# Expert down products of an MoE layer: weight tiles standing in two 64-column halves, the result transposed back by TensorE

## The chip, the cores and the metric

The kernel runs on one core of one Trainium2 chip. The metric is the device time of one execution in microseconds (us). TensorE is called PE below, its weight loads PEld, VectorE DVE, ScalarE ACT, GpSimd POOL and SyncE SP. "The queue" is the chain of DMA transfers that SP issues.

## The reference

Two layers of a decoder trunk over 256 tokens of width 1024, all in float32. Each layer mixes tokens (a gated DeltaNet half and a stick-breaking attention half, which the change doesn't touch) and then mixes channels: a dense SwiGLU in layer 0, and in layer 1 eight expert SwiGLUs of width 3584, of which each token uses two.

```python
def swiglu(x, w_gate, w_up, w_down):
    return (jax.nn.silu(x @ w_gate) * (x @ w_up)) @ w_down

def moe_swiglu(h, router_w, w_gate, w_up, w_down):
    ...
    logits = (xt @ router_w).astype(jnp.float32)
    top_val, top_idx = lax.top_k(logits, TOP_K)
    gates = jax.nn.softmax(top_val, axis=-1)
    combine = jnp.einsum("nk,nke->ne", gates, jax.nn.one_hot(top_idx, N_EXPERTS, dtype=jnp.float32))
    y = jnp.zeros((B * T, D), dtype=jnp.float32)
    for e in range(N_EXPERTS):
        y = y + combine[:, e:e + 1] * swiglu(xt, w_gate[e], w_up[e], w_down[e]).astype(jnp.float32)
    return y.reshape(B, T, D).astype(h.dtype)
```

The three weight matrices of an expert hold 3 x 1024 x 3584 float32 values, 44 MB; all eight together 352 MB, and every one of them is read.

## The kernel before

The program is written engine by engine, with semaphores between them. Layer 0, the mixer of layer 1 and the router take the first 40% of the time. Then the experts run, in the order of their number. Each expert gets up to 96 tokens (`SLOTS`); if some expert had more, another round over all experts would follow, which happens once here.

**Gather.** `gather` builds the expert's input transposed, `xgT` (eight blocks of 128 features by 96 tokens), as products of three bf16 parts of the activations with one-hot matrices; DVE scales and copies it out of PSUM in `gathered`.

**Chunks.** The expert's width is cut in 14 chunks (`MOE_CH`) of 256 hidden features (`FC`). One chunk's weights are 1 MB each of gate, up and down (`load_ffn`, three transfers). They land in a ring of four slots (`NSLOT`). SP issues the loads of chunk n once the semaphore `ring_used` says that chunk n-4 has been used up, that is, once its down products are done.

**Gate and up, `m_gate_up`.** Weights stand, activations move: a 128 x 64 piece of the weights is the standing operand and the 96 tokens of `xgT` the moving one. The two 64-column halves of a 128-column weight tile go to the two halves of the PE's columns (`for lo in (0, P // 2)`). That makes 64 calls of a chunk. A float32 call is carried out as two MATMUL instructions, each with its LDWEIGHTS, so a chunk has 128 pairs. The result is the hidden layer transposed: features on partitions, 96 tokens along the row.

**Activation.** ACT takes silu of the gate half (L1132), DVE multiplies with the up half (L1505) into `moe_hid`, which is double buffered.

**Down, `m_down`.** Here it is the other way round: the hidden layer (128 features x 96 tokens) stands, and the down weights move, 512 columns at a time:

```python
ins = mm(bank(2 + half)[0:SLOTS, :], moe_hid[c % 2][:, i, :],
         d[:, i, half * 512:(half + 1) * 512], ...)
```

That is four calls, eight MATMULs of 512 columns, in a chunk. The sums of all 14 chunks pile up in PSUM banks 2 and 3, with tokens on 96 partitions and 1024 output features along the row.

**Order on PE.** `expert` runs gate/up of chunk c, then down of chunk c-1, so that ACT and DVE have the time of one down to make the next hidden tile. After gate/up of the last chunk comes the gather of the next expert, then the last down. ACT and DVE then each copy one bank of the result to `y_tok` (`y_copy`, L1125 and L1489), and after gate/up of the next expert's chunk 0, `scatter` spreads the 96 rows back to the 256 token rows by a product with a one-hot matrix (L873, four calls). DVE multiplies with the gate and adds (`accumulate`, L1494).

**Loop.** Expert 0 and expert 7 are written out; between them a loop of three rounds has two experts in its body. The chain of engines at the end of the program is: last `y_copy`, `scatter`, `accumulate`, then norm, residual and the store of the output.

Of the kernel before, what the change touches and what calls it, by code (L numbers as in the profile page):

```python
# [30 lines left out]
P = 128  # L31
D = 1024
# [84 lines left out]
def build(nc, x_in, consts, norm_mix_pre, norm_mix_post, norm_ffn_pre, norm_ffn_post, w_in, conv_w,  # L117
          dn_a_log, dn_dt_bias, dn_norm_w, sb_norm_w, w_out, ffn_gate, ffn_up, ffn_down, router_w,
          moe_gate, moe_up, moe_down, out):
    with ExitStack() as ctx:  # L120
# [90 lines left out]
        def cols(n):  # L211
# [37 lines left out]
        y_tok = BM[0:SLOTS, D:2 * D]  # L249

# [46 lines left out]
            sem(n) for n in ("mgu_ps", "msg_ready", "mhid_ready", "y_act", "y_dve", "scatter_ps"))  # L297
        moe_acc = [sem(f"moe_acc{t}") for t in range(TT)]
# [139 lines left out]
        def _(pe):  # L438
# [413 lines left out]
            def m_down(it, j, c, tail=False):  # L852

                d = gate_up_down(FIRST_MOE + j * MOE_CH + c)[2]
                pe.wait_ge(mhid_ready, it * (2 * MOE_CH) + (j * MOE_CH + c + 1))
                if tail and c == 0:
                    pe.wait_ge(y_act, it * 2 + j)
                    pe.wait_ge(y_dve, it * 2 + j)
                for i in range(FC // P):
                    for half in range(2):  # L860
                        ins = mm(bank(2 + half)[0:SLOTS, :], moe_hid[c % 2][:, i, :],  # L861
                                 d[:, i, half * 512:(half + 1) * 512],
                                 start=(c == 0 and i == 0), stop=(c == MOE_CH - 1 and i == 1))
                ins.then_inc(ring_used, 1)

# [11 lines left out]
            def expert(it, j, tail, nxt):  # L877

                for c in range(MOE_CH):
                    m_gate_up(it, j, c)  # L880
                    if c:
                        m_down(it, j, c - 1, tail)
                    if tail and c == 0:
                        scatter(*tail)
                if nxt:
                    if tail:
                        for t in range(TT):
                            pe.wait_ge(moe_acc[t], it * 2 + j)
                    gather(*nxt)
                m_down(it, j, MOE_CH - 1)  # L890
# [3 lines left out]
            with pe.Fori(0, rounds) as r:  # L894
# [9 lines left out]
                for t in range(TT):  # L904
                    pe.wait_ge(moe_acc[t], last * 2 + 1)
                scatter(last, 1)
# [5 lines left out]
        def _(act):  # L912
# [208 lines left out]

            def y_copy(it, j):

                act.wait_ge(ring_used, it * (2 * MOE_CH) + (FIRST_MOE + (j + 1) * MOE_CH))
                A(y_tok[:, 0:512], bank(2)[0:SLOTS, :], ACT.Copy).then_inc(y_act, 1)  # L1125

            def expert(it, j, tail, nxt):
                for c in range(MOE_CH):
                    act.wait_ge(mgu_ps, it * (2 * MOE_CH) + (j * MOE_CH + c + 1))
                    if c >= 2:  # L1130
                        act.wait_ge(mhid_ready, it * (2 * MOE_CH) + (j * MOE_CH + c - 1))
                    A(moe_sg[c % 2], bank(c % 2)[:, 0:2 * SLOTS].rearrange("p (a b) -> p a b", a=2),  # L1132
                      ACT.Silu).then_inc(msg_ready, 1)
                if nxt:
                    onehotT_copy(*nxt)
                y_copy(it, j)

            with act.Fori(0, rounds) as r:
# [8 lines left out]
                expert(last, 1, (last, 0), None)  # L1147
            for t in range(TT):
# [5 lines left out]
        def _(dve):  # L1154
# [331 lines left out]

            def y_copy(it, j):
                dve.wait_ge(ring_used, it * (2 * MOE_CH) + (FIRST_MOE + (j + 1) * MOE_CH))
                V.tensor_copy(y_tok[:, 512:D], bank(3)[0:SLOTS, :]).then_inc(y_dve, 1)  # L1489
# [10 lines left out]
            def expert(it, j, tail, nxt, nxt_e):  # L1500
                for c in range(MOE_CH):
# [6 lines left out]
                    if tail and c == 0:  # L1508
                        accumulate(*tail)
# [4 lines left out]
                y_copy(it, j)  # L1514

            with dve.Fori(0, rounds) as r:
# [9 lines left out]
                expert(last, 1, (last, 0), None, None)  # L1526
                accumulate(last, 1)
# [180 lines left out]
```

## Time and profile before

| | us |
|---|---|
| three runs: median (lowest to highest) | 1779.08 (1778.29 to 1780.57) |
| the profiled execution, its own time | 1775.79 |
| its span, first to last instruction | 1773.9 |
| PE busy | 1720.2 (97% of the span) |
| PE weight loads busy | 1268.8 (72%) |
| DVE, ACT, POOL busy | 283.3, 197.6, 143.5 |

The time of the profiled execution is 1.9 us more than its span, and 3.3 us less than the median of the three runs. The mean granted clock of TensorE is 0.982 of full speed. A busy PE is no proof of a PE at its peak: the instructions overlap, and what matters is the distance from one start to the next. The DMA share is the mean busy share of the core's 16 DMA engines as the profile counts their packets; it can read slightly over 1 when packets overlap.

### The profile page before, as it was taken

The numbers are of one execution on the slowest core, as the hardware profiler recorded it, in microseconds if no ns is written. First come the engines' busy times: TensorE is split into PE (matmuls) and PEld (weight loads), VectorE is DVE, ScalarE is ACT, GpSimd is POOL, SyncE is SP. The second block draws the span as 40 slices with busy tenths as digits, with TensorE's granted clock in tenths as the row PEclk, the third lists the DMA queues.
The fourth block names the chain that finished last, engine by engine and source line by source line (L and its number), as shares of the span: only waits on it lengthen the run. The fifth ranks groups of instructions, "written<-read, shape, count | busy, mean of one in ns | idle before, by whom it ended". The sixth has DMA issues, their size and how long they took to land.

```text
span 1773.9 us, 41158 instructions
## 1 busy us (share of the span) xinstructions
PE 1720.2 (97%) x18812; PEld 1268.8 (72%) x18812; DVE 283.3 (16%) x553; ACT 197.6 (11%) x462; POOL 143.5 (8%) x164
## 2 busy tenths in 40 slices
PE   7999999999999995999999999999999999999997
PEld 6788577777778755777777776777776777777774
DVE  2333310000434334001001001001001001001002
ACT  3123220000322323000000000000000000000000
POOL 2233200000123322000000000000000000000000
PEclk9999999999999996999999999999999999999999
DMA  8213244443320324999999999899899899899892
GB/s 308 73 46 120 95 152 168 168 153 132 122 102 27 119 95 143 308 350 341 315 350 333 322 351 326 296 349 353 304 350 346 278 348 352 303 352 354 298 353 97
DMA packets 311445, 432.58 MB, mean 244 GB/s; under 512 B 9051, under 2 KB 263261, under 8 KB 311277
## 3 DMA queue, kind: packets, MB, share of 16 engines
q1 hardware_dynamic: 310396, 427.75, 69.9%
q8 instruction: 150, 2.46, 0.6%
q0 software_dynamic: 672, 2.14, 0.4%
q10 hardware_dynamic: 208, 0.08, 0.0%
q14 instruction: 19, 0.15, 0.0%
HBM read 428.90 MB, written 1.05 MB: 242 GB/s over the span
## 4 chain that ended last, share of the span: by engine, by line
PE 94%; DVE 2%; ACT 1%; issue 1%; POOL 1%; SPq 0%; DMA 0%; DVEq 0%
PE ps L848 34%; PE ps L861 23%; PE ps L751 8%; PE ps L488 7%; PE ps L762 3%; PE ps L629 3%; PE ps L497 3%; PE ps L873 2%; PE ps L600 1%; PE ps L615 1%; PE ps L826 1%; PE ps L611 1%; PE ps L621 1%; PE ps L512 1%; PE ps L519 1%
## 5 line engine op out<-in xcount | busy, mean ns | idle before, releaser
L848 PEld LDWEIGHTS ps<-bv_sb,ring 128*64 128x64 f32 x14336 | 598.1, 137 | 92.6 <-issue 92.6
L848 PE MATMUL ps<-bv_sb,ring 128*64 128x96 f32 x14336 | 619.0, 247 | 6.2 <-issue 5.6
L861 PE MATMUL ps<-ring,LT_sb 128*96 128x512 f32 x896 | 410.9, 601 | 0.0
L861 PEld LDWEIGHTS ps<-ring,LT_sb 128*96 128x96 f32 x896 | 137.0, 163 | 191.6 <-issue 179.3
L1505 DVE TENSOR_TENSOR LT_sb<-LT_sb,ps 128x192 f32<-128x192 f32 x112 | 39.7, 354 | 916.8 <-ACT LT_sb L1132 916.8
L751 PE MATMUL ps<-hT_sb,ring 128*128 128x256 f32 (+1 forms) x768 | 155.7, 362 | 0.0
L751 PEld LDWEIGHTS ps<-hT_sb,ring 128*128 128x128 f32 x768 | 136.0, 190 | 24.6 <-issue 9.1
L1132 ACT ACTIVATE LT_sb<-ps 128x192 f32<-128x192 f32 x112 | 37.0, 330 | 948.9 <-PE ps L848 948.9
L488 PE MATMUL ps<-hT_sb,ring 128*128 128x256 f32 x608 | 139.4, 388 | 0.0
L488 PEld LDWEIGHTS ps<-hT_sb,ring 128*128 128x128 f32 x608 | 117.6, 196 | 17.0 <-DVE qk_sb L1220 0.5
L1556 POOL TENSOR_SCALAR small<-small 128x1 f32<-128x1 f32 x16 | 4.1, 254 | 1346.3 <-ACT XT_sb L951 1320.5
L762 PE MATMUL ps<-ring,LT_sb 128*128 128x512 f32 x144 | 64.7, 592 | 0.0
L629 PE MATMUL ps<-ring,hT_sb 128*128 128x512 f32 x128 | 56.7, 593 | 1.7 <-ACT hT_sb L1080 1.7
L497 PE MATMUL ps<-ring,hT_sb 128*128 128x512 f32 x128 | 56.9, 592 | 0.0
L762 PEld LDWEIGHTS ps<-ring,LT_sb 128*128 128x128 f32 x144 | 27.4, 190 | 26.8 <-issue 25.8
L1610 POOL TENSOR_TENSOR BM<-LT_sb,cst 128x512 f32<-128x512 f32 x28 | 37.9, 1365 | 73.5 <-DVE LT_sb L1310 40.5
L629 PEld LDWEIGHTS ps<-ring,hT_sb 128*128 128x128 f32 x128 | 23.5, 190 | 28.0 <-issue 28.0
L497 PEld LDWEIGHTS ps<-ring,hT_sb 128*128 128x128 f32 x128 | 23.7, 190 | 25.9 <-issue 25.8
L1409 DVE TENSOR_TENSOR LT_sb<-AT_sb,ps 128x256 f32<-128x256 f32 x22 | 9.3, 421 | 200.2 <-ACT AT_sb L1092 200.2
L1092 ACT ACTIVATE AT_sb<-ps 128x256 f32<-128x256 f32 x22 | 8.4, 383 | 198.4 <-PE ps L751 198.4
L873 PE MATMUL ps<-BM,X_sb 96*128 96x512 f32 x64 | 29.6, 605 | 0.9 <-DVE BM L1489 0.9
L1220 DVE SCALAR_TENSOR_TENSOR qk_sb<-ps,prm,qk_sb 128x255 f32<-128x255 f32 (+2 forms) x48 | 23.1, 481 | 31.0 <-ACT qk_sb L991 29.9
(259 smaller groups left out, 1002.9 us busy)
## 6 DMA issues: line engine op xcount, KB each, us to landing
ring<-in_moe_w_gate SPq DMA_DIRECT2D x112, 1024.0 KB, 5.9
ring<-in_moe_w_up SPq DMA_DIRECT2D x112, 1024.0 KB, 8.9
ring<-in_moe_w_down SPq DMA_DIRECT2D x112, 1024.0 KB, 10.8
ring<-in_ffn_w_gate SPq DMA_DIRECT2D x11, 1024.0 KB, 5.3
ring<-in_ffn_w_up SPq DMA_DIRECT2D x11, 1024.0 KB, 7.9
ring<-in_ffn_w_down SPq DMA_DIRECT2D x11, 1024.0 KB, 9.8
ring<-in_w_in SPq DMA_DIRECT2D x14, 768.0 KB, 6.4
ring<-in_w_out SPq DMA_DIRECT2D x8, 768.0 KB, 5.5
```

The source lines that it names most:

```text
L488: ins = mm(o[:, 0:T], w[:, k, col:col + P], hT[:, k, :], start=(k == 0), stop=(k == KD - 1))
L497: ins = mm(o, hT[:, k, i * P:(i + 1) * P], w[:, k, col:col + 512], start=(k == 0), stop=(k == KD - 1))
L629: ins = mm(bank(4 + 2 * t + hf), mixT[:, k, t * P:(t + 1) * P], w[:, k, :], start=(k == 4), stop=(k == 3))
L751: ins = mm(bank(mt % 4)[:, which * T + lo:which * T + hi], w[:, k, i * P:(i + 1) * P], hT[:, k, lo:hi], start=(k == 0), stop=(k == KD - 1))
L762: ins = mm(bank(4 + 2 * t + half), ffn_hid[:, mt % 4, t * P:(t + 1) * P], d[:, i, half * 512:(half + 1) * 512], start=(mt == 0), stop=(mt ...
L848: ins = mm(o[lo:lo + P // 2, :], w[:, k, i * P + lo:i * P + lo + P // 2], xgT[:, k, :], start=(k == 0), stop=(k == KD - 1))
L861: ins = mm(bank(2 + half)[0:SLOTS, :], moe_hid[c % 2][:, i, :], d[:, i, half * 512:(half + 1) * 512], start=(c == 0 and i == 0), stop=(c = ...
L873: ins = mm(bank((6, 4)[t] + half), onehotT[j][:, t * P:(t + 1) * P], y_tok[:, half * 512:(half + 1) * 512], start=True, stop=True)
L1132: A(moe_sg[c % 2], bank(c % 2)[:, 0:2 * SLOTS].rearrange("p (a b) -> p a b", a=2), ACT.Silu).then_inc(msg_ready, 1)
L1220: V.scalar_tensor_tensor(conv_dst(m)[:, s:T], bank(step_bank(m + 1))[:, 0:T - s], prm[:, w:w + 1], conv_dst(m)[:, s:T], ALU.mult, ALU.add)\
L1505: V.tensor_tensor(moe_hid[c % 2], moe_sg[c % 2], bank(c % 2)[:, 2 * SLOTS:4 * SLOTS].rearrange("p (a b) -> p a b", a=2), ALU.mult).then_in ...
L1610: G.tensor_tensor(BT[:, s, :], LT[:, s, :], bcm(cst[:, C_LVL + l * P:C_LVL + (l + 1) * P], 4), ALU.mult).then_inc(BT_ready, 1)
```

## The change

The down products take the form of the gate/up products. Each 128 x 64 piece of the down weights stands, in two 64-column halves, and the 96 tokens of `moe_hid` move. Eight blocks of 128 output features times two halves times two feature tiles make 32 calls, 64 MATMULs of 96 columns, in a chunk, instead of 8 of 512 columns. The sums pile up transposed: banks 2 and 3 hold four blocks each of 128 output features by 96 tokens.

The scatter still wants tokens on partitions. So at an expert's end ACT and DVE copy banks 2 and 3 to a new view `yT` of the tile `hT_sb` (`yT_copy`), PE transposes the eight blocks into banks 4 and 5 (`y_transposes`, after gate/up of chunk 0 of the next expert), and ACT and DVE copy those to `y_tok`. The scatter comes one chunk later than before, behind the down of chunk 0, and DVE's accumulation with it. The last expert does all of it in a row.

```diff
+        yT = v3(hT_sb, KD, 0, KD * SLOTS)
...
                 if tail and c == 0:
-                    pe.wait_ge(y_act, it * 2 + j)
-                    pe.wait_ge(y_dve, it * 2 + j)
+                    pe.wait_ge(yT_act, it * 2 + j)
+                    pe.wait_ge(yT_dve, it * 2 + j)
                 for i in range(FC // P):
-                    for half in range(2):
-                        ins = mm(bank(2 + half)[0:SLOTS, :], moe_hid[c % 2][:, i, :],
-                                 d[:, i, half * 512:(half + 1) * 512],
-                                 start=(c == 0 and i == 0), stop=(c == MOE_CH - 1 and i == 1))
+                    for m in range(KD):
+                        o = bank(2 + m // 4)[:, m % 4 * SLOTS:(m % 4 + 1) * SLOTS]
+                        for lo in (0, P // 2):
+                            ins = mm(o[lo:lo + P // 2, :], d[:, i, m * P + lo:m * P + lo + P // 2], moe_hid[c % 2][:, i, :],
+                                     start=(c == 0 and i == 0 and m % 4 == 0), stop=(c == MOE_CH - 1 and i == 1),
+                                     skip_group_check=True)
                 ins.then_inc(ring_used, 1)
+
+            def y_transposes(it, j):
+
+                pe.wait_ge(yT_act, it * 2 + (j + 1))
+                pe.wait_ge(yT_dve, it * 2 + (j + 1))
+                for m in range(KD):
+                    ins = nc.tensor.transpose(bank(4 + m // 4)[0:SLOTS, m % 4 * P:(m % 4 + 1) * P], yT[:, m, :], ident)
+                ins.then_inc(yT_ps, 1)
...
                     if tail and c == 0:
+                        y_transposes(*tail)
+                    if tail and c == 1:
                         scatter(*tail)
...
+                y_transposes(last, 1)
                 scatter(last, 1)
...
+            def yT_copy(it, j):
+
+                act.wait_ge(ring_used, it * (2 * MOE_CH) + (FIRST_MOE + (j + 1) * MOE_CH))
+                A(yT[:, 0:4, :], bank(2)[:, 0:4 * SLOTS].rearrange("p (a b) -> p a b", a=4), ACT.Copy).then_inc(yT_act, 1)
+
             def y_copy(it, j):
 
-                act.wait_ge(ring_used, it * (2 * MOE_CH) + (FIRST_MOE + (j + 1) * MOE_CH))
-                A(y_tok[:, 0:512], bank(2)[0:SLOTS, :], ACT.Copy).then_inc(y_act, 1)
+                act.wait_ge(yT_ps, it * 2 + (j + 1))
+                A(y_tok[:, 0:512], bank(4)[0:SLOTS, :], ACT.Copy).then_inc(y_act, 1)
...
+            def yT_copy(it, j):
+                dve.wait_ge(ring_used, it * (2 * MOE_CH) + (FIRST_MOE + (j + 1) * MOE_CH))
+                V.tensor_copy(yT[:, 4:8, :], bank(3)[:, 0:4 * SLOTS].rearrange("p (a b) -> p a b", a=4)).then_inc(yT_dve, 1)
...
                     if tail and c == 0:
+                        y_copy(*tail)
+                    if tail and c == 1:
                         accumulate(*tail)
```

PE's own order at the start of an expert, before. L848 is gate/up, L873 the scatter, L861 the down product; counts are calls, each two MATMULs.

```order
L898 UNCONDITIONAL_BRANCH
L898 ISA
L839 ISA
L848 MATMUL ps<-bv_sb,ring 64x96 x64
L868 ISA
L873 MATMUL ps<-BM,X_sb 128x512 x4
L848 MATMUL ps<-bv_sb,ring 64x96 x64
L855 ISA
L861 MATMUL ps<-ring,LT_sb 96x512 x4
L848 MATMUL ps<-bv_sb,ring 64x96 x64
```

The same place on PE after the change. L850 is gate/up, L875 the transposes, L865 the down product, L885 the scatter.

```order
L912 UNCONDITIONAL_BRANCH
L912 ISA
L841 ISA
L850 MATMUL ps<-bv_sb,ring 64x96 x64
L872 ISA
L875 MATMUL ps<-cst,hT_sb 96x128 x8
L850 MATMUL ps<-bv_sb,ring 64x96 x64
L857 ISA
L861 REGISTER_ALU
L865 MATMUL ps<-LT_sb,ring 64x96 x32
L885 MATMUL ps<-BM,X_sb 128x512 x4
L850 MATMUL ps<-bv_sb,ring 64x96 x64
```

The four calls of a down product have become 32, and the scatter has moved from before the gate/up of chunk 1 to behind the down of chunk 0, so the slot of chunk 0 is given back ahead of the scatter.

## Rows read from the trace of the kernel before

**Rows 1.** The page: PE's busy tenths and the DMA share in 40 slices.

```profile
PE   7999999999999995999999999999999999999997
DMA  8213244443320324999999999899899899899892
```

**Rows 2.** The page: the chain that ended last, by line.

```profile
PE ps L848 34%; PE ps L861 23%; PE ps L751 8%; PE ps L488 7%; PE ps L762 3%; PE ps L629 3%; PE ps L497 3%; PE ps L873 2%; PE ps L600 1%; PE ps L615 1%; PE ps L826 1%; PE ps L611 1%; PE ps L621 1%; PE ps L512 1%; PE ps L519 1%
```

**Rows 3.** The page: costliest groups (count, then busy us, mean ns, then idle before).

```profile
L848 PEld LDWEIGHTS ps<-bv_sb,ring 128*64 128x64 f32 x14336 | 598.1, 137 | 92.6 <-issue 92.6
L848 PE MATMUL ps<-bv_sb,ring 128*64 128x96 f32 x14336 | 619.0, 247 | 6.2 <-issue 5.6
L861 PE MATMUL ps<-ring,LT_sb 128*96 128x512 f32 x896 | 410.9, 601 | 0.0
```

**Rows 4.** The waits of SP, the issuer of the loads (total, times, longest).

```profile
SPq L402 <- PE ps L861: 680.8, 108, 34.8
```

**Rows 5.** Timeline of one chunk in mid-expert (start, length, engine, group).

```profile
1004.64 5.50 PE L848 MATMUL ps<-bv_sb,ring 128*64 128x96 f32 x128
...
1004.88 0.37 SPq L402 DMA_DIRECT2D ring<-in_moe_w_gate  x1
...
1010.08 3.67 PE L861 MATMUL ps<-ring,LT_sb 128*96 128x512 f32 x8
...
1010.64 0.35 DVE L1505 TENSOR_TENSOR LT_sb<-LT_sb,ps 128x192 f32<-128x192 f32 x1 [8.68 <-ACT LT_sb L1132]
...
1013.68 5.50 PE L848 MATMUL ps<-bv_sb,ring 128*64 128x96 f32 x128
```

**Rows 6.** Timeline, PE: the first two gate/up blocks of expert 0, back to back.

```profile
698.96 10.78 PE L848 MATMUL ps<-bv_sb,ring 128*64 128x96 f32 x256 [0.63 <-DVE bv_sb L1483]
```

**Rows 7.** Timeline, PE: a change of experts inside the loop body.

```profile
1224.40 3.62 PE L861 MATMUL ps<-ring,LT_sb 128*96 128x512 f32 x8
1227.95 5.50 PE L848 MATMUL ps<-bv_sb,ring 128*64 128x96 f32 x128
1233.38 3.70 PE L873 MATMUL ps<-BM,X_sb 96*128 96x512 f32 x8
1237.02 5.50 PE L848 MATMUL ps<-bv_sb,ring 128*64 128x96 f32 x128
```

**Rows 8.** Timeline, PE: the first gate/up block behind the loop's branch back.

```profile
1094.42 6.90 PE L848 MATMUL ps<-bv_sb,ring 128*64 128x96 f32 x128 [2.77 <-issue]
```

**Rows 9.** Windows (engines' busy us, then PE clock, DMA share, GB/s).

```profile
1088.00:1104.00 16.00, 13.22 (x147) 9.22 (x145) 2.33 (x4) 1.30 (x3) 0.00 (x0) 0.89 1.08 371
1005.00:1077.00 72.00, 72.00 (x1088) 52.00 (x1085) 2.83 (x8) 2.64 (x8) 0.00 (x0) 1.00 1.02 350
```

**Rows 10.** A load onto an idle queue: issue, first data (window), landing of its last part.

```profile
1114.15 0.37 SPq L402 DMA_DIRECT2D ring<-in_moe_w_gate  x1
...
1115.00:1116.00 1.00, 1.00 (x30) 1.00 (x28) 0.00 (x0) 0.00 (x0) 0.00 (x0) 1.00 0.62 143
...
L404 SPq DMA_DIRECT2D ring<-in_moe_w_down x1: 1062/1062/1062, 1115.3 to 1115.3; - x1
...
DMA to landing us min/median/max: 10.6/10.6/10.6
```

**Rows 11.** The third parts of two loads queued one behind the other, with their landing.

```profile
L404 SPq DMA_DIRECT2D ring<-in_moe_w_down x1: 3217/3217/3217, 1492.6 to 1492.6; - x1
...
DMA to landing us min/median/max: 11.7/11.7/11.7
...
L404 SPq DMA_DIRECT2D ring<-in_moe_w_down x1: 3657/3657/3657, 1500.5 to 1500.5; - x1
...
DMA to landing us min/median/max: 13.6/13.6/13.6
```

**Rows 12.** Timeline, PE: four transposes in the mixer.

```profile
641.26 0.60 PE L635 MATMUL ps<-cst,h_sb 128*128 128x128 f32 x4
```

**Rows 13.** Timeline, PE: the last scatter of the program.

```profile
1759.78 3.67 PE L873 MATMUL ps<-BM,X_sb 96*128 96x512 f32 x8 [0.87 <-DVE BM L1489]
```

More of the change, by code:

```diff
@@ L297, in build @@
             sem(n) for n in ("mgu_ps", "msg_ready", "mhid_ready", "y_act", "y_dve", "scatter_ps"))
+        yT_act, yT_dve, yT_ps = (sem(n) for n in ("yT_act", "yT_dve", "yT_ps"))
         moe_acc = [sem(f"moe_acc{t}") for t in range(TT)]
@@ L1133, in expert @@
                       ACT.Silu).then_inc(msg_ready, 1)
+                    if tail and c == 0:
+                        y_copy(*tail)
                 if nxt:
                     onehotT_copy(*nxt)
-                y_copy(it, j)
+                yT_copy(it, j)
             with act.Fori(0, rounds) as r:
@@ L1147, in _ @@
                 expert(last, 1, (last, 0), None)
+                y_copy(last, 1)
             for t in range(TT):
@@ L1485, in gathered @@
                                     bcl(wffn[:, 4 * b:4 * b + 4], SLOTS), ALU.mult).then_inc(xg_ready, 1)
+            def yT_copy(it, j):
+                dve.wait_ge(ring_used, it * (2 * MOE_CH) + (FIRST_MOE + (j + 1) * MOE_CH))
+                V.tensor_copy(yT[:, 4:8, :], bank(3)[:, 0:4 * SLOTS].rearrange("p (a b) -> p a b", a=4)).then_inc(yT_dve, 1)
             def y_copy(it, j):
-                dve.wait_ge(ring_used, it * (2 * MOE_CH) + (FIRST_MOE + (j + 1) * MOE_CH))
-                V.tensor_copy(y_tok[:, 512:D], bank(3)[0:SLOTS, :]).then_inc(y_dve, 1)
+                dve.wait_ge(yT_ps, it * 2 + (j + 1))
+                V.tensor_copy(y_tok[:, 512:D], bank(5)[0:SLOTS, :]).then_inc(y_dve, 1)
             def accumulate(it, j):
@@ L1508, in expert @@
                     if tail and c == 0:
+                        y_copy(*tail)
+                    if tail and c == 1:
                         accumulate(*tail)
@@ L1513, in expert @@
                     gathered(*nxt)
-                y_copy(it, j)
+                yT_copy(it, j)
             with dve.Fori(0, rounds) as r:
@@ L1526, in _ @@
                 expert(last, 1, (last, 0), None, None)
+                y_copy(last, 1)
                 accumulate(last, 1)
```

## The prediction

> **What bounds the kernel now.** I read the slices first: from slice 17 on, the experts' part, PE is at 9 tenths and so is the DMA share [rows 1]. Two resources look full, so the question is which one PE would meet if it got faster. The chain that ended last is PE alone there, 34% gate/up (L848) and 23% down (L861) [rows 2]. PE hardly waits: the 14336 gate/up MATMULs have 6.2 us of idle time before them in all, the down MATMULs 0.0 [rows 3]. SP on the other hand waits 680.8 us, 108 times, for down products to free a slot [rows 4]. So PE bounds this part and the loads follow it.
>
> The timeline gives a chunk's price. Gate/up starts at 1004.64, down at 1010.08, the next gate/up at 1013.68 [rows 5]: 5.44 + 3.60 = 9.04 us. Two gate/up blocks back to back take 10.78 us for 256 MATMULs [rows 6]; less the 0.25 us of a single one that is 10.53 / 255 = 41.3 ns from start to start, 5.28 us for 128. The other 0.16 us of the 5.44 is the turn from 64-column tiles to full width.
>
> The loads: a window with two loads queued moves 371 GB/s at a share of 1.08, the mid-expert window 350 GB/s at 1.02 [rows 9]. A chunk is 3.146 MB. At 371 GB/s it takes 8.48 us, and PE asks for one every 9.04 us. The queue has 6% to spare and no more. That is the number to keep in view.
>
> **The change, part by part.**
>
> *Down products.* 64 MATMULs of 96 columns replace 8 of 512. No row shows this operation, but gate/up has its exact form: 128 x 64 standing, 96 moving, two halves in turn. The near end is 41.3 ns each: 64 x 41.3 ns = 2.64 us in place of 3.60. Both turns of tile width go too. The far end is a pair of halves that don't overlap, 82.5 ns each, 5.28 us. I take 41.3, since only the order of the output regions differs. A chunk then costs PE 192 x 41.3 ns = 7.92 us, 1.12 less. Over 112 chunks that would be 125 us.
>
> The standing operand is where a rule speaks against the change. The row: 14336 weight loads keep PEld busy for 598.1 us [rows 3], 41.7 ns each, no slower than the MATMULs. The Trainium skill (TensorE: Matmul & The Clock Gate, section LDWEIGHTS) puts a weight load at its columns over 1.2 GHz, 53 ns for 64 columns; one after another, 192 of them would make a chunk 10.2 us and the kernel slower than before by some 130 us as an estimate. The trace disagrees for the same form already, so the sum doesn't use it.
>
> *Cover of the hidden tile.* DVE ends at 1010.99, 0.91 us behind the start of down [rows 5]; down still covers this with 2.64 us.
>
> *Change of experts.* Before: an expert inside the loop body lasts 1227.95 - 1094.42 [rows 7, 8] = 133.53 us, 1.47 of which is the first block's slowness behind the branch (6.90 against the usual 5.43). 132.06 less 14 x 9.04 leaves 5.5: the scatter takes 3.64 (1233.38 to 1237.02 [rows 7]) and the gather some 2.0. Added are eight transposes. Four take 0.60 us [rows 12], so 0.11 us each; eight cost 0.9, with their turns of width and latency I take 1.4 (bounds 0.9 and 2.5). The `yT` copies lie beside the 5.28 us of gate/up of chunk 0, the `y_tok` copies beside that of chunk 1; each is one pass of ACT and DVE under 0.7 us, free unless gate/up shrank below that. DVE's accumulation moves behind the down of chunk 0; waiting for it are hid 2 (covered by the next gate/up) and the next gather, ten chunks later. SP has no more to issue than before. PE's work of an expert becomes 14 x 7.92 + 2.0 + 3.6 + 1.4 = 118.0 us, for 132.1.
>
> *Branch back.* The loop goes back twice, with 2.77 us idle and 1.47 us of slow start [rows 8]; the granted clock of that window is 0.89 against 1.00 elsewhere [rows 9], some of it at the lower level, 1.2 GHz, behind the idle time. I keep 4.3 each.
>
> *The loads.* They were hidden; now they aren't. 14 x 8.48 = 118.7 us of queue time for an expert stands against 118.0 of PE, and the two don't fall together: in mid-expert the queue needs 8.5 for each 7.92 of PE, and at a change PE is busy elsewhere while the ring is full. What I need is the queue's pace over a long full stretch, which the trace shows for two loads at most. The low bound is 8.48. Of eight such couples the landings lie 8.4 to 8.7 us apart in six; one of the two others is 1492.6 + 11.7 = 1504.3 and 1500.5 + 13.6 = 1514.1, 9.8 apart [rows 11]. All eight average 8.9. The upper bound is 9.04, the pace it keeps today. I take 8.6, near the six, a little up for stragglers and for the instructions that PE fetches through the same engines, 192 pairs a chunk where there were 136.
>
> *The sum of the expert part.* If the queue never rests: first slot free at 698.96 + 2 x 5.28 + 2.64 = 712.2. From there to first data 1.6 us: 0.24 from the last down to SP's issue [rows 5], and some 1.3 from issue to data (1114.15, data from about 1115.4 [rows 10]). 108 loads x 8.6 = 928.8, to 1642.6. From there to landing 1.9: this load took 1115.3 + 10.6 - 1114.15 = 11.8 us in all [rows 10], less 1.3 and 8.6. Behind the last landing one gate/up and two downs, 10.6. Total 1655.1.
>
> Does the queue rest? Only at a change of experts, where slots come free late. Count from the landing of chunk 13. The next load began 1.9 earlier, and four are on order (slots freed by downs 10 to 13), so the queue is full until 4 x 8.6 - 1.9 = 32.5, and with the one behind them until 41.1. PE does gate/up 13, down 12, gather, down 13 (12.6), then gate/up 0, transposes, gate/up 1, down 0 (14.6, at 27.2: in time), then scatter, gate/up 2, down 1 (11.6, at 38.7), data 1.6 later at 40.3. That is 0.8 to spare, and a branch back of 4.3 us costs 3.5, twice. The last down ends at 1662.1.
>
> The PE-only sum for comparison: 699.0 + 112 x 7.92 + 7 x 7.0 + 8.6 = 1643.7. The queue is later. Within an expert PE runs ahead first: a load onto an idle queue takes 12.1 us of the 15.8 that two chunks of PE give it, and the 3.7, with what the pause at the change adds, are used up at 0.7 us a chunk. Then PE waits.
>
> *The end.* Before, the copies start at 1758.94 (0.84 before the scatter [rows 13]), one us behind the last down, and 15.0 us follow. Now comes one more hop of 0.87, eight transposes of 0.11, and latency: 2.3 us (bounds 1.8 and 4, since PE may have fallen to the lower clock). Span: 1662.1 + 1.0 + 15.0 + 2.3 = 1680.4. With 1.9 us around it the profiled execution would take 1682.3. The median stood 3.3 above the profiled time, so **1685.6 us**, 5.3% less. The 125 us of PE shrink to 93: the queue takes the rest.
>
> **The rivals.**
>
> *A, the queue keeps up.* Its pace is 8.4 or better over a long stretch, PE stays the bound, with the 1643.7 from above: 1643.7 + 18.3 + 5.2 = 1667. For it: 371 GB/s is the mean of a window with dips, and single microseconds read up to 410. Against: a share of 1.08 already. The Trainium skill (HBM Reference, section Specifications) says that a core streaming alone measures about 425 GB/s, 7.4 us a chunk; by that the ring would never run dry and A would be the outcome. Rows 9 show 371 with all engines busy.
>
> *B, the queue is slower than it looks.* At 8.9 us, the mean of the eight couples, 108 x 0.3 = 32 more than the forecast: 1718. At 9.04 it is 108 x 0.44 = 48 more: 1733.
>
> *C, the halves don't overlap, slower than before.* Place: `m_down`, where each half changes its output region at every call, within one PSUM bank, while gate/up stays on a region for eight calls. If that stops the overlap, down costs 5.28 and a chunk 10.56: 112 x 1.52 = 170 more, 7 x 1.4 + 2.3 = 12 more, 1961 us. It turns from gain to loss where the down MATMULs stand more than (9.04 - 0.11 - 5.28) / 64 = 57 ns apart. For it: no row shows alternating regions. Against: the halves alternate in gate/up too and their pace is the streaming time.
>
> *D, no real gain:* that pace at about 57 ns, within 4 us of 1779.
>
> **How the numbers follow.** Forecast 0.57, A 0.17, B 0.19, C 0.05, D 0.02. The likeliest is 1685. The range runs from A with a little off, 1664, to the 8.9 of B, 1720; C, D, the far part of B and a queue with no bound at all stay outside, about 0.15. About 0.2% is what a measurement of this kernel can tell from no change. Faster has 0.94, same 0.01, slower 0.05.
>
> **What would show it.** Right: in mid-expert the issues of L402 stand 8.5 to 8.7 us apart (9.04 before) in the last chunks of an expert and 7.9 in the first ones; PE idles some 0.6 us a chunk before gate/up there, the DMA share has no dips; down MATMULs are 64 in 2.64 us; two stops of 2.8 us at the branch. A would show no idle time before gate/up and dips in GB/s. B shows the idle time in over half of each expert's chunks. C shows down blocks of over 5 us and a DMA share of 0.85. Most in doubt is the queue's pace: 0.1 us there is 10 us of the total.

## The result: 0.35% slower, and the profile after

| | before | after |
|---|---|---|
| median (lowest to highest), us, 5 runs each | 1780.12 (1778.29 to 1780.92) | 1786.53 (1780.79 to 1788.51) |
| profiled execution, its own time; its span | 1775.79; 1773.9 | 1780.79; 1779.0 |
| PE busy, us | 1720.2 | 1637.5 |
| mean granted clock | 0.982 | 0.983 |

The ratio is 1.0035, 95% interval 1.0023 to 1.0046. The forecast was 1685.6 us, with a range of 1664 to 1720. PE has 82.7 us less to do, and the kernel gained nothing. From the page of the changed kernel, the parts that answer to [rows 1], [rows 2] and [rows 3], and the line of the instruction queue (packets, MB, share of the DMA engines):

```profile
PE 1637.5 (92%) x25148; PEld 1441.5 (81%) x25148; DVE 287.7 (16%) x561; ACT 201.5 (11%) x470; POOL 143.4 (8%) x164
...
PE   8999999999999995998998998988998988999996
...
DMA  8213244443320324999999999899899799899893
...
q8 instruction: 201, 3.29, 0.8%
...
PE 90%; issue 6%; DVE 2%; ACT 1%; POOL 1%; DMA 0%; DVEq 0%
...
L850 PE MATMUL ps<-bv_sb,ring 128*64 128x96 f32 x14336 | 634.4, 247 | 38.7 <-issue 37.5
...
L865 PE MATMUL ps<-LT_sb,ring 128*64 128x96 f32 x7168 | 332.7, 247 | 53.0 <-issue 52.9
```

The down MATMULs were 410.9 us with no idle time [rows 3] and are 332.7 us with 53.0. The digits of PE have fallen to 8 in many slices, while DMA has stayed at 9. And the idle time is ended by "issue": PE waited for nothing that the profile shows, no load, no hidden tile, no copy. PE's waits, longest totals first (us in total, times, longest):

```profile
PE ps L865 <- issue: 52.9, 42, 1.9
PE ps L850 <- issue: 37.5, 35, 6.0
```

That is 90.4 us against 5.6 before [rows 3], 84.8 more: it eats the 82.7 that PE saved. No wait for a DMA stands in the list; that alone doesn't clear the weights, since "issue" only says that the profile shows nothing that PE waited for (a run below has waits for weights under that name). The timeline of PE shows where the stops lie:

```profile
748.44 1.07 PE L865 MATMUL ps<-LT_sb,ring 128*64 128x96 f32 x21 [1.34 <-issue]
749.32 0.25 PE L850 MATMUL ps<-bv_sb,ring 128*64 128x96 f32 x1
749.34 0.25 PE L865 MATMUL ps<-LT_sb,ring 128*64 128x96 f32 x1
749.40 5.38 PE L850 MATMUL ps<-bv_sb,ring 128*64 128x96 f32 x126
754.60 0.25 PE L865 MATMUL ps<-LT_sb,ring 128*64 128x96 f32 x1
754.62 0.25 PE L850 MATMUL ps<-bv_sb,ring 128*64 128x96 f32 x1
754.68 2.74 PE L865 MATMUL ps<-LT_sb,ring 128*64 128x96 f32 x62
757.24 0.25 PE L850 MATMUL ps<-bv_sb,ring 128*64 128x96 f32 x1
757.26 0.25 PE L865 MATMUL ps<-LT_sb,ring 128*64 128x96 f32 x1
757.32 5.64 PE L850 MATMUL ps<-bv_sb,ring 128*64 128x96 f32 x126
762.80 0.25 PE L865 MATMUL ps<-LT_sb,ring 128*64 128x96 f32 x1
762.80 0.25 PE L850 MATMUL ps<-bv_sb,ring 128*64 128x96 f32 x1
762.88 1.82 PE L865 MATMUL ps<-LT_sb,ring 128*64 128x96 f32 x39
765.76 1.21 PE L865 MATMUL ps<-LT_sb,ring 128*64 128x96 f32 x24 [1.06 <-issue]
```

A stop falls in the middle of a down product, between two calls that wait for nothing. Add the counts from one stop to the next: 21 + 1 + 1 + 126 + 1 + 1 + 62 + 1 + 1 + 126 + 1 + 1 + 39 = 382. The stop before was at 730.79, 381 MATMULs earlier. Each MATMUL has its LDWEIGHTS beside it, so that is 3 x 256 instructions, less a few waits and register steps. Other stops stand about 254 or 127 MATMULs apart. The instruction queue moved 3.29 MB in 201 packets, 16.4 KB each (2.46 MB before): 256 instructions of 64 bytes. **PE stops where one such block of its own program ends and the next has not come.**

The trace also has the time of each of these packets. The one before the last stop above lies between 763.21 and 764.30, on the queue's line of that window (763.0 to 764.4; packets, MB, share of 16 engines), and PE goes on at 765.76:

```profile
q8 instruction: 1, 0.02, 4.9%
```

It is so at every stop. Of the changed kernel's stops in the experts' part, 80 last over 0.1 us, 92.2 us together, and each of the 80 ends 1.2 to 1.7 us behind the last byte of such a packet. But for the two at the branches back, none of them stands at an instruction that waits for a semaphore. The ring of weights, which I had named, is not what PE waited for. Between the stops all is as forecast: down blocks of 64 MATMULs without a stop last 2.64 us.

The Trainium skill (Runtime: NRT & Kernel Launch, section Instruction fetch mechanics) describes this machinery: instructions come in 16 KiB blocks of 256 over a DMA queue that the sequencer drives itself, the next block during the current one, at a cost that is "mostly hidden". The sizes agree with this trace. "Hidden" does not: 90.4 us of idle time here, against 5.6 in the kernel before. The page's other rule, that a taken branch breaks the fetch ahead, agrees with the loop's branches back, the longest stops of both traces (2.77 us [rows 8], 6.0 after).

**Two theories to test.** Theory F: PE's program blocks arrive late when it uses them fast and the DMA engines are full of weights. Theory W: it is the weights after all, as forecast, or a part of a load that lands late, and "issue" is only how the profile books it. The packet times above speak for F in this trace; the runs show what it depends on. The expectations name a third theory, that the new form stops PE by itself; the first run tests it. The measure used below is the time that PE took for a block of 128 pairs: the window 740 to 820 us (first expert, no branch) divided by its MATMUL count over 128. The window holds no whole number of chunks, so the figure is good to some 2%. In the changed kernel:

```profile
740.00:820.00 80.00, 72.00 (x1691) 70.11 (x1687) 3.19 (x9) 2.97 (x9) 0.00 (x0) 1.00 1.04 357
```

80.00 / (1691 / 128) = 6.06 us a block, where PE's own pace is 128 x 41.3 ns = 5.3 us.

### The profile page after: what moved, and what is told of

It reads as the page before. It is cut to its first block, busy times and chain, and to the rows that moved or that the text cites. A ratio compares the mean times of both kernels' runs of the same rounds, so it can differ in the third digit from the quotient of the medians.

```text
span 1779.0 us, 53862 instructions
## 1 busy us (share of the span) xinstructions
PE 1637.5 (92%) x25148; PEld 1441.5 (81%) x25148; DVE 287.7 (16%) x561; ACT 201.5 (11%) x470; POOL 143.4 (8%) x164
## 3 DMA queue, kind: packets, MB, share of 16 engines
q8 instruction: 201, 3.29, 0.8%
## 4 chain that ended last, share of the span: by engine, by line
PE 90%; issue 6%; DVE 2%; ACT 1%; POOL 1%; DMA 0%; DVEq 0%
PE ps L850 34%; PE ps L865 17%; PE ps L753 8%; PE ps L490 7%; PE ps L764 3%; PE ps L631 3%; PE ps L499 3%; PE ps L885 2%; PE ps L602 1%; PE ps L617 1%; PE ps L828 1%; PE ps L613 1%; PE ps L623 1%; PE ps L458 1%; PE ps L514 1%
## 5 line engine op out<-in xcount | busy, mean ns | idle before, releaser
L850 PE MATMUL ps<-bv_sb,ring 128*64 128x96 f32 x14336 | 634.4, 247 | 38.7 <-issue 37.5
L850 PEld LDWEIGHTS ps<-bv_sb,ring 128*64 128x64 f32 x14336 | 611.6, 138 | 57.7 <-issue 56.8
L865 PE MATMUL ps<-LT_sb,ring 128*64 128x96 f32 x7168 | 332.7, 247 | 53.0 <-issue 52.9
L865 PEld LDWEIGHTS ps<-LT_sb,ring 128*64 128x64 f32 x7168 | 312.2, 137 | 59.4 <-issue 58.3
L631 PE MATMUL ps<-ring,hT_sb 128*128 128x512 f32 x128 | 56.7, 594 | 1.7 <-ACT hT_sb L1095 1.7
L885 PE MATMUL ps<-BM,X_sb 96*128 96x512 f32 x64 | 29.6, 605 | 0.9 <-DVE BM L1516 0.9
```

What stands on the lines that cost most here:

```text
L631: ins = mm(bank(4 + 2 * t + hf), mixT[:, k, t * P:(t + 1) * P], w[:, k, :], start=(k == 4), stop=(k == 3))
L850: ins = mm(o[lo:lo + P // 2, :], w[:, k, i * P + lo:i * P + lo + P // 2], xgT[:, k, :], start=(k == 0), stop=(k == KD - 1))
L865: ins = mm(o[lo:lo + P // 2, :], d[:, i, m * P + lo:m * P + lo + P // 2], moe_hid[c % 2][:, i, :], start=(c == 0 and i == 0 and m % 4 == 0 ...
L885: ins = mm(bank((6, 4)[t] + half), onehotT[j][:, t * P:(t + 1) * P], y_tok[:, half * 512:(half + 1) * 512], start=True, stop=True)
```

## The experiments

Each ratio is against the kernel before, on the same chip, with its 95% interval.

### Loads cut to an eighth

Every expert load brings only its first eighth (one of eight blocks of gate and up, 128 of 1024 columns of down), so the DMA engines are nearly empty and PE's program is the same.

```diff
-                        load_ffn(n, moe_gate[0, e][:, f], moe_up[0, e][:, f], moe_down[0, e][f, :])
+                        sp_.dma_start(g[:, 0:1, :], wg.rearrange("(k p) f -> p k f", p=P)[:, 0:1, :]).then_inc(s, 16)
+                        sp_.dma_start(u[:, 0:1, :], wu.rearrange("(k p) f -> p k f", p=P)[:, 0:1, :]).then_inc(s, 16)
+                        sp_.dma_start(d[:, :, 0:128], wd.rearrange("(i p) d -> p i d", p=P)[:, :, 0:128]).then_inc(s, 16)
```

> The changed kernel with the expert loads cut to an eighth (the rest of each ring slot keeps old values, so the expert sums are of other weights); every instruction of PE, ACT and DVE as before. Three theories. Code fetch: PE's own instructions come in blocks of 16 KB, 256 instructions, 128 pairs or 5.3 us at full pace, and a block takes up to 7 us to come when the DMA engines are full of weights. Weights: PE waits for late weights. Form: the new down products or their order stop PE by themselves. Code fetch expects no stops inside the down blocks, 7.9 us a chunk, about 1668 us. Weights expects the same 1668. Form expects the stops to stay, about 1785.

Measured: 1665.5 us, ratio 0.9355 (0.9330 to 0.9381). PE's wait for issue, the window, and the timeline:

```profile
PE ps L855 <- issue: 5.9, 2, 3.1
```

```profile
740.00:820.00 80.00, 80.00 (x1931) 79.69 (x1927) 4.86 (x12) 3.87 (x12) 0.00 (x0) 1.00 0.19 56
```

```profile
746.04 5.48 PE L855 MATMUL ps<-bv_sb,ring 128*64 128x96 f32 x128
751.32 2.84 PE L870 MATMUL ps<-LT_sb,ring 128*64 128x96 f32 x64
753.96 5.48 PE L855 MATMUL ps<-bv_sb,ring 128*64 128x96 f32 x128
```

The chunk is 753.96 - 746.04 = 7.92 us, to the hundredth what the form was costed at. Only the two branches back still stop PE. So the new form does give the whole gain, and the weight traffic takes it away; a form that stops PE by itself is ruled out. The run by itself doesn't tell delayed weights from delayed instructions. It also prices the loss: 1779.0 - 1664.7 = 114.3 us of span, of which 90.4 - 5.9 = 84.5 are stops and 1637.5 - 1609.4 = 28.1 are MATMULs that count as busy for longer. Some 15 of these 28 us belong to the same stops: the last MATMUL before a stop counts as busy for 0.25 us, where the next one else starts after 0.04, so each of the 75 stops beyond the branches back hides about 0.2 us. The other 13, such as the 5.64 us for 126 MATMULs in the timeline of the changed kernel against 5.48 for 128 here, have no cause shown.

### Only the down loads cut

Gate and up whole, down to an eighth: the weights need 2.125 of 3 MB, some 70% of the queue.

```diff
+                        sp_.dma_start(g[:, 0:8, :], ...)
+                        sp_.dma_start(u[:, 0:8, :], ...)
+                        sp_.dma_start(d[:, :, 0:128], wd.rearrange("(i p) d -> p i d", p=P)[:, :, 0:128]).then_inc(s, 16)
```

> The changed kernel with only the down weights' load cut to an eighth (old values in the rest), so the DMA engines have two thirds of their work. Weights expects no wait left, 1668 us, since 2.2 MB a chunk need 6 us of the queue. Code fetch expects what depends on when a block is asked for: while weights stream some stops stay, 1675 to 1730. Form expects 1785.

Measured: 1760.9 us, ratio 0.9891 (0.9864 to 0.9919). Waits, and the window:

```profile
PE ps L870 <- issue: 45.8, 38, 1.9
PE ps L855 <- issue: 29.9, 32, 5.9
```

```profile
740.00:820.00 80.00, 70.64 (x1660) 68.87 (x1657) 3.19 (x9) 2.97 (x9) 0.00 (x0) 1.00 0.76 243
```

The loads now ask for 243 GB/s where 357 is shown possible, and PE still stops for 75.7 us, at 6.17 us a block. This speaks against W, which expected no wait: weights that need 70% of the queue shouldn't be late, and all stops over 0.1 us end 1.2 to 1.7 us behind an instruction packet again. A share of 0.76 is enough to delay the instruction blocks. The time lies above F's own range as well: I had thought that fewer weights would help more.

### Empty instructions in the kernel before

The reverse test: the old form, with waits on a semaphore that is already set put behind each of the four calls of a down product, 56 as written. That is 224 in a chunk, not the 112 of the expectation; but the instruction queue moved 201 packets (150 before), some 116 more instructions a chunk, so a chunk has about 192 pairs' worth, as meant.

```diff
+                        for _ in range(56):
+                            pe.wait_ge(params_ps, 1)
```

> The kernel before the change with 112 empty instructions on PE in each chunk's down products (waits for a semaphore that was met long ago), so that its PE code is as long as the changed kernel's, 1.5 blocks of 256 a chunk, with its MATMULs as they were. Code fetch expects stops to appear in a kernel that has none, 20 to 90 us slower than 1780. Weights and form expect 1780, unless the empty instructions themselves lengthen the down blocks evenly.

Measured: 2915.5 us, ratio 1.638 (1.635 to 1.642). Inconclusive. The eight MATMULs of a down product are torn apart by gaps of 1.2 to 2.1 us, one at each batch of waits, and the mean granted clock is 0.792 (0.982 before). It says nothing on F, only that a satisfied wait is no empty instruction.

### Down with whole 128-column tiles

The same orientation with fewer instructions: 16 calls of 128 standing columns instead of 32 of 64; 160 pairs a chunk.

```diff
-                        o = bank(2 + m // 4)[:, m % 4 * SLOTS:(m % 4 + 1) * SLOTS]
-                        for lo in (0, P // 2):
-                            ins = mm(o[lo:lo + P // 2, :], d[:, i, m * P + lo:m * P + lo + P // 2], moe_hid[c % 2][:, i, :],
...
+                        ins = mm(bank(2 + m // 4)[:, m % 4 * SLOTS:(m % 4 + 1) * SLOTS], d[:, i, m * P:(m + 1) * P],
+                                 moe_hid[c % 2][:, i, :],
```

> The changed kernel with the down weights standing in one full 128-column tile in place of two 64-column halves: 32 MATMULs a chunk in place of 64, PE's code a sixth shorter (160 pairs a chunk, 192 before). If they stream at 82 ns, a chunk is 5.44 + 2.64 + 0.16 = 8.24 us of PE and code fetch expects few stops, 1700 to 1730 us. If each 128-column weight load holds PE up by 107 ns, a chunk is 9.0 and the time 1780 to 1790 with no stops at all. Weights expects the time of the changed kernel, 1786, either way.

Measured: 1813.1 us, ratio 1.0186 (1.0163 to 1.0208).

```profile
1010.39 5.50 PE L850 MATMUL ps<-bv_sb,ring 128*64 128x96 f32 x128
1015.82 3.81 PE L863 MATMUL ps<-LT_sb,ring 128*128 128x96 f32 x32
1019.56 5.50 PE L850 MATMUL ps<-bv_sb,ring 128*64 128x96 f32 x128
```

```profile
740.00:820.00 80.00, 80.00 (x1419) 78.09 (x1419) 2.86 (x9) 2.98 (x9) 0.00 (x0) 1.00 1.01 344
```

No stop within an expert, with the DMA engines full (13.9 us of waits for issue in four stops, each at a branch back or at the block behind it). But a pair of 128 standing columns takes 3.74 / 32 = 117 ns, nearly three times the 41.3, and the chunk is 9.17 us. The weight load is the bound of this form: PEld is busy 78.09 of 80 us. The Trainium skill (TensorE: Matmul & The Clock Gate, section LDWEIGHTS) puts a load at its columns over 1.2 GHz; worked out for 128 columns that is an estimate of 107 ns. This run, with 117, nearly agrees; the 64-column halves, 41.3 ns by the trace and 53 by the rule, don't. The kernel is slower than any theory expected of it (1786 to 1790 us at most), and this run decides nothing between F and W.

### The loads in another shape

Three runs change how the loads arrive and leave PE's products alone; PE's waits name other semaphores in the first and the third. In the first every 1 MB load is issued in four pieces of 256 KB.

```diff
+                    for k in range(0, KD, 2):
+                        sp_.dma_start(dst[:, k:k + 2, :], src[:, k:k + 2, :]).then_inc(moe_landed[x % NSLOT], 16)
...
+                    for h in range(2):
+                        sp_.dma_start(d[:, i, half(h)], src[:, i, half(h)]).then_inc(moe_landed[x % NSLOT], 16)
```

> The changed kernel with each 1 MB load issued as four of 256 KB, same bytes and rows (1 KB rows for gate and up; 2 KB rows for the pieces of down). Code fetch, turn by turn: if a DMA engine serves a code block only between one load's bundle of packets and the next, quarter bundles let it in four times as soon, the stops go, and the time falls to where the weights bound it, 1665 to 1710 us. Code fetch, plain crowding: the block shares memory and wires with the same bytes as before and nothing changes, 1780 to 1790. SP's 12 issues of 0.4 to 0.5 us fit in 7.9 us, so no cost from them.

Measured: 1760.2 us, ratio 0.9898 (0.9881 to 0.9914). Waits for issue 58.0 and 16.7 us, 6.03 us a block. The time lies between the two that were expected.

In the second gate and up are read in rows of 4 KB instead of 1 KB. They are other elements of the same matrices, four stretches of each in turn; the bytes are as many.

```diff
+                            big = src[0, e].rearrange("(a p) f -> p a f", p=P)[:, :, 0:1024]
+                            sp_.dma_start(dst.rearrange("p k f -> p (k f)").rearrange("p (a f) -> p a f", a=2),
+                                          big[:, 2 * c4:2 * c4 + 2, :]).then_inc(s, 16)
```

> The changed kernel with gate and up loaded from rows of 4 KB in place of 1 KB, the same bytes (other values of the weights, so the expert sums are of other weights). If the 1 KB packets are what crowds the code blocks out, the stops shrink: 1665 to 1720 us. If the bytes alone count, 1780 to 1790. The pace of the queue at full stretch shows too: 371 GB/s if nothing depends on the row, more if it does.

Measured: 1742.9 us, ratio 0.9801 (0.9782 to 0.9821). The best loads of the three, and still:

```profile
PE ps L872 <- issue: 30.1, 41, 1.4
PE ps L857 <- issue: 28.2, 27, 5.9
```

Its window has 363 GB/s at a share of 0.95, and 5.85 us a block. The Trainium skill (HBM Reference, section Specifications) gives 425 GB/s for a core alone; no long window here shows it: 4 KB rows reach 381 over 72 us, and 1 KB rows 371 over 16 us [rows 9]. The time again lies between the two that were expected.

In the third SP issues a part only when the second part before it has landed, so that two transfers are on order at most, and each part has a semaphore of its own.

```diff
+                            m, r = divmod(3 * x + k - 2, 3)
+                            if m >= 0:
+                                sp_.wait_ge(part_landed[r][m % NSLOT], uses(m))
+                            sp_.dma_start(dst, src).then_inc(part_landed[k][x % NSLOT], 16)
```

> The changed kernel with SP issuing a part only when the second part before it has landed, so that 2 MB at most stand in the queue (up to 4 now), and PE waiting for down weights only before down. If the delay of a code block is the length of the queue ahead of it, the stops shrink, and the time is 1680 to 1730 us, bounded by the slightly starved queue. If it is crowding by whatever streams, the time is 1780 to 1800.

Measured: 1762.3 us, ratio 0.9898 (0.9858 to 0.9939), between the two expectations too. Waits for issue 56.7 and 16.6 us, 6.12 us a block. Not all of them are instructions. From 1449 us on, 20 stops (20.8 us) stand before a whole gate/up block and end 0.1 us behind the landing of that chunk's up weights:

```profile
1572.91 5.50 PE L879 MATMUL ps<-bv_sb,ring 128*64 128x96 f32 x128 [1.56 <-issue]
1578.22 2.84 PE L895 MATMUL ps<-LT_sb,ring 128*64 128x96 f32 x64
1582.38 5.50 PE L879 MATMUL ps<-bv_sb,ring 128*64 128x96 f32 x128 [1.32 <-issue]
```

Here the ring does run dry, as W has it, and the profile books it as "issue" all the same. In the change no stop is of this kind. Until 1440 us, where the ring is ahead, the stops come to 50.4 us, in the change to 67.9. Each of the three shapes gives 1 to 2%, none the 6% of the empty engines.

### Half of the features in the new form

If F holds, the quantity to watch is the time PE takes for a block, and a version between the two forms should have the gain without the stops. Output features 0 to 511 go the new way (16 calls), 512 to 1023 the old (2 calls): 164 pairs a chunk. Bank 3 holds tokens on partitions again, so four transposes fall away with one `y_copy` of DVE.

```diff
-                    for m in range(KD):
+                    for m in range(KD // 2):
...
+                for i in range(FC // P):
+                    ins = mm(bank(3)[0:SLOTS, :], moe_hid[c % 2][:, i, :], d[:, i, 512:1024],
+                             start=(c == 0 and i == 0), stop=(c == MOE_CH - 1 and i == 1))
...
-                V.tensor_copy(yT[:, 4:8, :], bank(3)[:, 0:4 * SLOTS].rearrange("p (a b) -> p a b", a=4)).then_inc(yT_dve, 1)
+                V.tensor_copy(y_tok[:, 512:D], bank(3)[0:SLOTS, :]).then_inc(y_dve, 1)
```

> Half of each way: output features 0 to 511 with standing weights (16 calls a chunk), 512 to 1023 as before the change (2 calls, the hidden layer standing). 164 pairs a chunk; PE 5.28 + 1.32 + 1.72 + 0.3 = 8.6 to 8.7 us a chunk. Code fetch: a block lasts 6.7 us on average and comes in time nearly always, so few stops: chunk 8.7, 4 transposes a change of experts, 1740 to 1755 us, faster than either kernel. Weights (a queue that can't go beyond today's 350 GB/s): 1780.

Measured: **1742.87 us (1742.64 to 1744.83), ratio 0.9801 (0.9784 to 0.9817)**, faster than both kernels.

```profile
1005.03 5.50 PE L850 MATMUL ps<-bv_sb,ring 128*64 128x96 f32 x128
1010.37 1.49 PE L865 MATMUL ps<-LT_sb,ring 128*64 128x96 f32 x32
1011.79 1.96 PE L869 MATMUL ps<-ring,LT_sb 128*96 128x512 f32 x4
1013.67 5.50 PE L850 MATMUL ps<-bv_sb,ring 128*64 128x96 f32 x128
```

```profile
PE ps L850 <- issue: 8.5, 2, 4.3
```

```profile
740.00:820.00 80.00, 80.00 (x1493) 65.94 (x1492) 3.19 (x9) 2.98 (x9) 0.00 (x0) 1.00 1.06 364
```

A chunk of 8.64 us, 6.7 us a block, PE busy through the window, and 364 GB/s of weights, more than the changed kernel drew (357). The two waits are the branches back. PE waits for no load here, so the queue can feed a chunk every 8.64 us: close to the 8.6 that the forecast had as an estimate.

### Three quarters of the features

Features 0 to 767 new, 768 to 1023 old (256 moving columns): 180 pairs, between the two.

```diff
-                    for m in range(KD):
+                    for m in range(6):
...
+                    ins = mm(bank(3)[0:SLOTS, 256:512], moe_hid[c % 2][:, i, :], d[:, i, 768:1024],
+                             start=False, stop=(c == MOE_CH - 1 and i == 1), skip_group_check=True)
```

> The change for output features 0 to 767, the old form for 768 to 1023 (four MATMULs with 256 moving columns). 128 + 48 + 4 = 180 pairs a chunk, between the 164 of the half version (8.64 us, no stops in a block) and the 192 of the change. PE's own work would be 5.28 + 48 x 0.0413 + 4 x 0.22 + turns 0.25 = 8.4 us, so a block of 128 pairs lasts 6.0 us, against 5.3 in the change and 6.7 in the half version. Theory of late instruction fetches (up to 7 us from asking to use with a full queue): stops come back, shorter or fewer, 20 to 60 us of idle time with issue as its releaser, 1740 to 1765 us, not faster than the half version. Rival, a threshold on the queue (PE stops only where it outruns the loads' pace of 8.5 us a chunk): no stops, chunks of 8.5 us, 1720 to 1735.

Measured: 1779.35 us (1770.58 to 1789.37, 12 runs), ratio 1.0004 (0.9986 to 1.0023). The profiled run is the slowest of the twelve.

```profile
PE ps L850 <- issue: 26.3, 20, 5.7
PE ps L865 <- issue: 17.8, 16, 1.9
...
PE ps L869 <- issue: 8.9, 7, 1.8
```

```profile
808.00 2.15 PE L865 MATMUL ps<-LT_sb,ring 128*64 128x96 f32 x48
810.08 1.10 PE L869 MATMUL ps<-ring,LT_sb 128*96 128x256 f32 x4
811.12 5.50 PE L850 MATMUL ps<-bv_sb,ring 128*64 128x96 f32 x128
816.45 2.15 PE L865 MATMUL ps<-LT_sb,ring 128*64 128x96 f32 x48
818.53 0.46 PE L869 MATMUL ps<-ring,LT_sb 128*96 128x256 f32 x1
820.33 0.81 PE L869 MATMUL ps<-ring,LT_sb 128*96 128x256 f32 x3 [1.34 <-issue]
```

The stops are back, 43 of them and 53.0 us (the two branches back among them), within the 20 to 60 expected, and the rival of a plain threshold on the weights' pace (no stops) has fallen. The total is 14 us above what I expected of it. Chunks without a stop take 8.45 us, 6.0 us a block (the gate/up before the lines shown starts at 802.67, the next at 811.12). Stops may also cost clock: between 1350 and 1450 us of this profile the granted clock averaged 0.93, part of it at the lower level, 1.2 GHz, where it was 0.98 in the changed kernel. The twelve runs spread over 19 us, the four of the half version over 2.

### The split loads on kernels without stops

Does the split help PE's instructions, or the loads as such? The same edit on the half version and on the kernel before.

> The half version (features 0 to 511 in the new form, 164 pairs a chunk) with each 1 MB load issued in four pieces. In the change itself the split took 20 us off. If it did that by letting PE's instruction blocks through sooner, it has nothing to take here, where PE has no stops in a block: 1738 to 1747 us, within 0.3% of the half version. Rival: the pieces speed up the weight loads themselves or the turn at a change of experts, whatever PE does: 10 to 20 us off here too, 1723 to 1733.

> The kernel before with each 1 MB load issued in four pieces. It has 3 stops of PE with issue as their releaser in the experts' part (6.5 us, two of them at the branch back). If the split only shortens waits for instructions: 1775 to 1782 us, same as before. Rival, the split speeds up something else: 10 to 20 us off, 1760 to 1770.

Measured: half version with split loads 1742.61 us, ratio 0.9804 (0.9791 to 0.9816), no different from the half version; the kernel before with split loads 1771.94 us, ratio 0.9965 (0.9952 to 0.9979). The first is what F expects: where no block is late, the split has nothing to take. The second is neither: 0.35% faster, less than the rival's 10 to 20 us but more than nothing. Where those 6 us come from is not shown; the two profiled spans differ by 1.3 us only (1773.9 and 1772.6), and PE waits 4.5 us for issue there.

### What the runs say together

| kernel | pairs a chunk | PE's own us a block | measured us a block | GB/s | stops |
|---|---|---|---|---|---|
| before | 136 | 8.5 | 8.4 | 349 | none |
| 128-column tiles | 160 | 7.3 | 7.2 | 344 | none |
| half | 164 | 6.7 | 6.9 | 364 | none |
| three quarters | 180 | 6.0 | 6.5 | 348 | yes |
| the change | 192 | 5.3 | 6.06 | 357 | yes |
| the change, split loads | 192 | 5.3 | 6.03 | 355 | yes |
| the change, two parts on order | 192 | 5.3 | 6.12 | 345 | yes |
| the change, 4 KB rows | 192 | 5.3 | 5.85 | 363 | yes |
| the change, down loads cut | 192 | 5.3 | 6.17 | 243 | yes |
| the change, loads to an eighth | 192 | 5.3 | 5.30 | 56 | none |

All of the window 740 to 820 us; "own" is the chunk without a stop over its pairs, times 128; "stops" leaves the branches back out. Where there are none, "own" and "measured" should agree, and do within the 2% of the window. PE stops in every kernel that would use a block in 6.0 us or less while the engines are three quarters full or more, and in none that takes 6.7 or longer. Where it is held, it gets a block every 5.9 to 6.5 us. For 192 pairs that is 1.5 x 6.06 = 9.1 us a chunk: by chance the 9.04 of before. Hence no gain. What is late is the start of the packet: the packet itself takes 1.09 us in the median, in the change and with the loads cut to an eighth alike.

## Why the prediction was wrong

**Right: the form.** Down products 64 x 41.3 ns = 2.64 us, a chunk of 7.92 us; the trace has both where nothing stops it. The sum with PE as the only bound, 1643.7 + 18.3 = 1662, stands against a span of 1664.7 with the loads cut to an eighth. Rivals C and D (halves that don't overlap, a pace of 57 ns) did not come about.

**Right, or off by little: the end and the change of experts.** Last down to last scatter grew by 1.8 us, estimated 2.3: the down ends at 1762.16 and the scatter starts at 1764.83, with 0.87 between the two before. Eight transposes cost 1.0 us (1105.39 to 1106.40), estimated 1.4.

**Off: the branch back.** I kept 4.3 us each. (Its 1.47 us of slow start sets a printed length, 6.90, against a distance of starts, 5.43; length against length, 6.90 - 5.50, is 1.40.) It became 5.98 idle and 7.64 to the next call instead of 5.28, 8.3 in all, twice: 8 us more. The idle part is a fetch too, and ends 1.7 us behind the landing of a 16 KB packet, in both kernels; the slow block runs at a granted clock of 0.70. The timeline of PE there, which answers to [rows 8]:

```profile
1097.75 7.71 PE L850 MATMUL ps<-bv_sb,ring 128*64 128x96 f32 x128 [5.98 <-issue]
1105.39 1.08 PE L875 MATMUL ps<-cst,hT_sb 128*96 128x128 f32 x8
1106.40 5.50 PE L850 MATMUL ps<-bv_sb,ring 128*64 128x96 f32 x128
```

**The step that failed** is the term for the loads: "I take 8.6, near the six, a little up for stragglers and for the instructions that PE fetches through the same engines, 192 pairs a chunk where there were 136." Instruction fetches were counted as a small load on the queue, within the 0.12 us between 8.48 and 8.6, and never as something that PE waits for. What they cost is their delay: PE needs the next block in 5.3 us, and behind a full set of engines it gets one every 6. The runs put 9.1 us a chunk in the place of 8.6, and PE waits for its program, not for the ring. The 8.6 as a pace of the weights is not what was wrong: the half version was fed a chunk every 8.64 us without a wait. So the case that came out, slower than before, had a chance of 0.05 for another reason, and the time lies 67 us above the top of the range.

**What could have been read.** The first block behind the loop's branch [rows 8] shows PE idle for 2.77 us: the price of one late block, in the profile before. The instruction queue of that profile moves 10 packets between 740 and 820 us, one in 8 us. Dividing PE's planned instructions by 256 would have given 5.3 us, and the question whether 5.3 is enough. The reading of [rows 1], "two resources look full", missed a third user of the full one.

**Open.** That the stops are late instruction blocks is shown by their spacing, by the packets that land 1.2 to 1.7 us before each of them ends, by the empty engines, by the cut down loads and by the three dosages. The test that would have added instructions to the old form failed. Why stops come at every second or third block is in part in the packets: between 748 and 766 us they start at 750.21, 756.66 and 763.21, 6.5 us apart, while PE uses a block in 5.3, so it starts each block with less in hand until it stops. Not shown are why the first packet behind a stop comes sooner, what in the DMA engines holds a packet of 1.09 us up, what makes up the last 13 us of the loss, and where the split loads find 0.35% in the kernel before.

## What to carry to other kernels

Count an engine's instructions as traffic with a deadline: 256 of them to a block, and the time in which the engine uses one block set against what a block takes under the load that the DMA engines have at that place (here about 6 us at full load, not noticed when 6.7 were given). Where a change trades few long MATMULs for many short ones beside a full weight stream, look for the share of work at which the two limits meet; half the change was worth 2.0% here, three quarters and all of it nothing. Idle time that ends with "issue" inside a run of identical calls is the sign to look for; where it stands at the first call of a block, compare it with the landing of the weights and of the instruction packets before naming the cause.

## What the runs showed that I had not expected

- PE's own program, 0.8% of the DMA engines' time, cost 84.5 us of stops out of 1779, and some 15 more that hide in them; the run with the loads cut is 114 us shorter in all.
- Less traffic helped little until there was almost none: 243 GB/s gave 6.17 us a block, 56 GB/s the 5.30 of PE itself.
- A batch of satisfied semaphore waits, 56 as written, leaves a gap of 1.2 to 2.1 us on PE.
- "Issue" can hide a wait for weights: 20 stops of the run with two parts on order.
- Whole 128-column standing tiles cost 117 ns a pair and two 64-column halves 2 x 41.3 = 82.6 ns, for the same products.
